# The wide matmuls of a two-layer decoder trunk walk their columns from the last to the first

## Chip, cores and metric

One core of one Trainium2 chip runs the whole program, two layers of a decoder trunk on a sequence of 256 tokens. The metric is device time in microseconds (us). Three runs of the kernel before took 861.75, 861.93 and 862.0 us.

## The reference

`x` is 256 x 1024 in float32. Each of two layers computes

```
h = RMSNorm(x)
[pool | diff-attn | stick-breaking | forgetting-attn | forget logits | gate logits] = h @ w_in      # 1024 x 7428
y_n = branch_n(...) @ w_branch[rows of branch n]                                                     # 1280 x 1024 in all
x = x + (sum_n sigmoid(gate_logit_n + b_gate_n) * y_n) @ w_out                                       # 1024 x 1024
x = x + (silu(gate) * up) @ w_down, with [gate | up] = RMSNorm(x) @ w_up                             # 1024 x 5632, 2816 x 1024
```

All weights are float32. The attention branches have four heads of 64 (the differential one four pairs, with values of 128).

## The kernel before

**Units.** The products with the five weight matrices are cut into items of up to 512 output columns, and the items into units: one unit is 2 x 128 weight rows by 512 columns (260 columns in the item `pf`). A layer has 144 units (`U`). The unit is the step of every pipeline: the load queue (SyncE) fetches it into one of 6 slots of `raw` (L562), ScalarE rounds it to the matmul's fp32r type in `w_hi` (L737), VectorE writes what the rounding left over into `w_lo` (L1013), both in rings of 5 slots, and TensorE multiplies it (`multiply`, L1668). Loads wait for `lo_ready` of the unit 6 earlier, ScalarE's copy waits for `unit_done` of the unit 5 earlier.

**Wide products.** The activations stand in SBUF turned (features on partitions) and split in the same manner into a rounded part and a rest (`hT`, `oT`, `aT`, each `_hi` and `_lo`). For each of the two weight row tiles of a unit and each of the two token tiles, `multiply` issues three matmuls into the same sums: high by high (L1692), high by low (L1693) and low by high (L1696). The activations are the stationary operand, 128 x 128, loaded anew for each matmul; the weights are streamed, and the output is 128 tokens by 512 columns of float32, a whole PSUM bank. `bulk` has four banks: two items by two token tiles, used in turn. The first four units, which start before all inputs are there, have their own order in `first_unit` (L1705), and the last unit's second token tile is done in two halves of 256 columns into the banks A and B (L1790 to L1792), so that the last additions and stores can start early.

**Order.** TensorE's order is written out by hand: before unit u the stages listed in `PE_TIMETABLE` run (transposes, attention scores, masks, sums), then the unit's twelve wide matmuls. Most units are multiplied singly; at four places four units are grouped so that all of tile 0 comes before tile 1. VectorE and ScalarE have tables of the same kind. They take the finished sums out of `bulk` after a semaphore that the last matmul of a unit or item raises (`unit_done`, `early_done`; for the residual sums L1057), and a bank is written afresh only after its reader's semaphore (`released_by`). At the end VectorE adds the two half banks to `x` (L1406) and ScalarE's queue stores the last piece (L996).

The small matmuls of the stages (transposes at L1441, L1634 and others, scores through `product_pair` at L1432, masks at L1576) are issued by lines of their own.

A bank's address comes from one line:

```python
        def item_bank(layer, n, t):
            return bulk[:, (layer * NITEM + n) % 2, t, :]
```

Of the kernel before, what the change touches and what calls it, by code (L numbers as in the profile page):

```python
# [32 lines left out]
P = 128  # L33
TT = 2
SEQ = TT * P
DEPTH = 2
D = 1024
KD = D // P
# [37 lines left out]
def item_k(n):  # L76
    k = ITEMS[n][3]
    return list(k) if not isinstance(k, int) else list(range(k))
# [23 lines left out]
U = len(UNITS)  # L102
# [207 lines left out]
def build(nc, x, attn_norm, ffn_norm, w_in, b_gate, w_branch, w_out, w_ffn_up, w_ffn_down, consts, params, turned_x, out):  # L310
# [8 lines left out]
    with ExitStack() as ctx:  # L319
        def sb(name, shape, dt=F32, stack=ctx, align=32):  # L320
            return stack.enter_context(nc.sbuf_tensor(name, shape, dt, align_bytes=align))
# [15 lines left out]
        def nth(semaphore, layer, event):  # L337

            order_in_layer = event_order[id(semaphore)]
            if layer == 0 and event in first_norm:  # L340
                return first_norm[event]
            return layer * len(order_in_layer) + order_in_layer[event] + more_in_first[id(semaphore)]
# [6 lines left out]
        w_hi = sb("w_hi", [P, RING, 2, NC], F32R, align=LINE)  # L349
        w_lo = sb("w_lo", [P, RING, 2, NC], F32R, align=LINE)  # L350

        x_sb = sb("x_sb", [P, TT, D])
        hT = [sb("hT_hi", [P, KD, SEQ], F32R, align=LINE), sb("hT_lo", [P, KD, SEQ], F32R, align=LINE)]
# [102 lines left out]
        def item_bank(layer, n, t):  # L456
            return bulk[:, (layer * NITEM + n) % 2, t, :]
# [76 lines left out]
        def released_by(name, t):  # L534

            return {
                "dq": (normed, ("dq", t)), "pf": (u_ready, t), "dk": (normed, ("dk", t)), "ss": (ss_staged, t),
                "svfq": (squares, ("fq", t)), "fkfv": (squares, ("fk", t)), "dv": (v_ready, ("dv", t)),
                "gate": (gate_ready, (name[1], t)), "branch": (gated, (*name[1:], t)),
                "out": (x_out, (t, name[1])), "down": (x_down, (t, name[1])),  # L540
                "ffg": (ff_gated, (name[1], t)), "ffu": (ff_ready, (name[1], t)), "fflast": (ff_ready, (NPAIR, t)),
            }[name if isinstance(name, str) else name[0]]
# [175 lines left out]
        def _(act):  # L718
# [226 lines left out]
            def nothing(*_):  # L945
                pass
# [463 lines left out]
        def _(pe):  # L1410
# [3 lines left out]
            def take(banks, *freed):  # L1414

                for b in banks:
# [2 lines left out]
                        pe.wait_ge(sig, nth(sig, layer, event))  # L1419
                    last_read[b] = freed  # L1420

            def product(dst, a, b, start, stop):

                pe.matmul(dst, a[0], b[0], start=start, stop=False, skip_group_check=True)
                pe.matmul(dst, a[0], b[1], start=False, stop=False, skip_group_check=True)
                return pe.matmul(dst, a[1], b[0], start=False, stop=stop, skip_group_check=True)
# [214 lines left out]
            def lhs_of(name, k, t):  # L1641

                kind = name if isinstance(name, str) else name[0]
                if kind == "branch":
                    event = (("pool", k) if k < 2 else ("diff", t) if k < 6 else ("sb", k - 6) if k < 8 else ("fox", k - 8))
                    return oT, event
                if kind == "down":
                    return aT, ("act", k // 4, t)
                if kind == "out":
                    return hT, ("merged", k // 4, t)  # L1650
                which = "ffn" if kind in ("ffg", "ffu", "fflast") else "attn"
                return hT, ("norm", which, t, k // 4)
# [9 lines left out]
            def wait_low(layer, event):  # L1662

                if nth(lhs_lo, layer, event) > reached["low"]:
                    reached["low"] = nth(lhs_lo, layer, event)
                    pe.wait_ge(lhs_lo, nth(lhs_lo, layer, event))

            def multiply(g, tiles, high=True, low=True):  # L1668

                layer, u = divmod(g, U)  # L1670
                n, k0 = UNITS[u]
                name, _, columns, _ = ITEMS[n]
                ks = item_k(n)
                width = sum(w for _, w in columns)
                fresh_bank = high and k0 == ks[0] and layer * NITEM + n >= 2
                before, m = divmod(layer * NITEM + n - 2, NITEM)
                for i in range(2):
                    k = k0 + i
                    whi, wlo = w_hi[:, g % RING, i, 0:width], w_lo[:, g % RING, i, 0:width]
                    for t in tiles:  # L1680
                        operand, event = lhs_of(name, k, t)
                        hi, lo = (part[:, k, t * P:(t + 1) * P] for part in operand)
                        dst = item_bank(layer, n, t)[:, 0:width]
                        if fresh_bank and i == 0:
                            sig, released = released_by(ITEMS[m][0], t)
                            pe.wait_ge(sig, nth(sig, before, released))
                        if high:
                            if low:
                                wait_low(layer, event)
                            else:  # L1690
                                wait_high(layer, event)
                            pe.matmul(dst, hi, whi, start=(k == ks[0]), stop=False)  # L1692
                            pe.matmul(dst, hi, wlo, start=False, stop=False)  # L1693
                        if low:
                            wait_low(layer, event)
                            ins = pe.matmul(dst, lo, whi, start=False, stop=(k == ks[-1] or g == DEPTH * U - 2 and i == 1 and t == 1))  # L1696
                if g == DEPTH * U - 2 and 1 in tiles:
                    ins.then_inc(all_but_last_done, 1)
                elif low and 1 in tiles:
                    ins.then_inc(unit_done, 1)  # L1700
                elif low and k == ks[-1]:
                    ins.then_inc(early_done, 1)


            def first_unit(u):  # L1705

                tiles = range(2 * u, 2 * u + 2)

                def high(k):

                    if k < 2:
                        pe.wait_ge(first_tile_hi, k + 1)
                    else:
                        pe.wait_ge(lhs_hi, k - 1)
                    if u < 2 and k == 2 * u:
                        pe.wait_ge(first_tile_ready, u + 1)
                    else:
                        pe.wait_ge(hi_ready, nth(hi_ready, 0, u))
                    for t in range(TT):
                        pe.matmul(item_bank(0, 0, t), hT[0][:, k, t * P:(t + 1) * P], w_hi[:, u, k % 2, :], start=(k == 0), stop=False)  # L1720

                def low(k):

                    pe.wait_ge(lhs_lo, k + 1)
                    for t in range(TT):
                        pe.matmul(item_bank(0, 0, t), hT[1][:, k, t * P:(t + 1) * P], w_hi[:, u, k % 2, :], start=False, stop=False)

                for k in tiles:
                    high(k)
                    if u < 2:  # L1730
                        low(k)
                if u >= 2:
                    for k in tiles:
                        low(k)
                pe.wait_ge(lo_ready, nth(lo_ready, 0, u))
                last = u == KD // 2 - 1
                for t in range(TT):
                    for k in tiles:
                        ins = pe.matmul(item_bank(0, 0, t), hT[0][:, k, t * P:(t + 1) * P], w_lo[:, u, k % 2, :], start=False,
                                        stop=k == KD - 1)  # L1740
                    if last and t == 0:
                        ins.then_inc(early_done, 1)
                ins.then_inc(unit_done, 1)
# [10 lines left out]
            for layer in range(DEPTH):  # L1754
                u = 0 if layer else GROUPS[0]
# [27 lines left out]
            for q in range(2):  # L1783
                columns = slice(q * NC // 2, (q + 1) * NC // 2)
                take("AB"[q], lhs_lo, DEPTH - 1, ("act", NPAIR, 1))
                dst = bank["AB"[q]][:, 0:NC // 2]
                for i in range(2):
                    hi, lo = (part[:, k0 + i, P:SEQ] for part in aT)
                    whi, wlo = w_hi[:, last % RING, i, columns], w_lo[:, last % RING, i, columns]
                    pe.matmul(dst, hi, whi, start=(i == 0), stop=False)  # L1790
                    pe.matmul(dst, hi, wlo, start=False, stop=False)
                    ins = pe.matmul(dst, lo, whi, start=False, stop=(i == 1))  # L1792
                ins.then_inc(last_columns_done, 1)


# [48 lines left out]
```

## Time and profile before

| | |
|---|---|
| median of three runs | 861.93 us (861.75 to 862.0) |
| span of the profiled execution | 859.8 us |
| the profiled execution's total | not given beside its span |
| granted TensorE clock, mean | 1.000 |
| busy: TensorE / weight loads / VectorE / ScalarE / GpSimd | 855.7 / 711.6 / 593.9 / 446.0 / 113.6 us |
| matmuls | 4246 |
| read from memory | 158.74 MB, 186 GB/s over the span |

The span goes from the first to the last instruction of one execution; the runs' times take in what lies around it. Busy time is time in which at least one instruction of an engine is in flight. A matmul's listed duration includes its way through the array, which overlaps the next matmul, so the rate of a dense stretch is read from the distance between starts. A granted clock of 1.000 stands for 2.4 GHz, 0.5 for 1.2 GHz.

### The profile page before, as it was taken

The page shows a single profiled execution, that of the slowest core. Times are in us where ns is not written, and L with a number is a line of the kernel's source. Part 1 is how long each engine was busy: PE and PEld are TensorE (multiplying, and loading weights), DVE is VectorE, ACT ScalarE, POOL GpSimd, SP SyncE. Part 2 cuts the span into 40 slices and gives each one's busy share as a digit, 9 for nine tenths or more (in the row PEclk, how much of TensorE's full clock was granted, in tenths as well). Part 3 has the DMA queues.
Part 4 walks back from the last instruction along what each step waited for, and adds up shares of the span by engine and source line. Part 5 has one row for each costly group of instructions (what it writes and reads, how often), then busy time and mean ns, then how long its engine had stood idle before and what let it go on. Part 6 is the DMA issues. An engine that isn't in the chain of part 4 may idle for free.

```text
span 859.8 us, 11140 instructions
## 1 busy us (share of the span) xinstructions
PE 855.7 (100%) x4246; PEld 711.6 (83%) x4246; DVE 593.9 (69%) x850; ACT 446.0 (52%) x646; POOL 113.6 (13%) x89
## 2 busy tenths in 40 slices
PE   9999999999999999999999999999999999999998
PEld 7888888888888888888888888888888888888887
DVE  7896967768777665564479768768696765565543
ACT  7567654854454444443364674558443644444431
POOL 0750101005401000000005401010063000000000
PEclk9999999999999999999999999999999999999999
DMA  9846656475657666555566465665665576665641
GB/s 343 290 150 190 200 175 183 148 228 180 188 184 236 190 195 190 182 185 189 162 186 178 119 195 158 196 197 162 205 196 179 151 234 183 185 190 177 195 147 50
DMA packets 87815, 160.53 MB, mean 187 GB/s; under 512 B 7505, under 2 KB 14161, under 8 KB 87761
## 3 DMA queue, kind: packets, MB, share of 16 engines
q1 hardware_dynamic: 87328, 159.16, 58.8%
q8 instruction: 34, 0.56, 0.3%
q10 hardware_dynamic: 432, 0.66, 0.2%
q14 instruction: 21, 0.16, 0.0%
HBM read 158.74 MB, written 1.05 MB: 186 GB/s over the span
## 4 chain that ended last, share of the span: by engine, by line
PE 93%; DVE 3%; DMA 2%; ACT 1%; SPq 1%; issue 0%; ACTq 0%
PE bulk L1692 28%; PE bulk L1696 28%; PE bulk L1693 28%; DMA raw<-in_w_in_dram 2%; DVE w_lo L1013 2%; PE bankAB L1432 1%; PE bankAB L1634 1%; PE bankT L1587 0%; PE bankAB L1576 0%; ACT w_hi L737 0%; PE bankAB L1441 0%; PE bankAB L1532 0%; PE bankO L1545 0%; PE bankT L1634 0%; PE bankO L1634 0%
## 5 line engine op out<-in xcount | busy, mean ns | idle before, releaser
L1013 DVE TENSOR_TENSOR w_lo<-raw,w_hi 128x1024 fp32r<-128x1024 f32 (+1 forms) x288 | 362.3, 1272 | 156.5 <-ACT w_hi L737 152.9
L737 ACT ACTIVATE w_hi<-raw 128x1024 fp32r<-128x1024 f32 (+1 forms) x286 | 297.7, 1049 | 245.3 <-PE bulk L1696 240.8
L1692 PE MATMUL bulk<-w_hi,hT_hi 128*128 128x512 f32 (+1 forms) x880 | 344.1, 391 | 0.2 <-DVE w_lo L1013 0.2
L1693 PE MATMUL bulk<-w_lo,hT_hi 128*128 128x512 f32 (+1 forms) x880 | 339.2, 385 | 0.0
L1696 PE MATMUL bulk<-w_hi,hT_lo 128*128 128x512 f32 (+1 forms) x880 | 336.5, 386 | 0.0
L1692 PEld LDWEIGHTS bulk<-w_hi,hT_hi 128*128 128x128 f32 x880 | 165.3, 188 | 33.2 <-DVE w_lo L1013 0.7
L1696 PEld LDWEIGHTS bulk<-w_hi,hT_lo 128*128 128x128 f32 x880 | 165.0, 188 | 33.4
L1693 PEld LDWEIGHTS bulk<-w_lo,hT_hi 128*128 128x128 f32 x880 | 165.4, 188 | 31.7
L1692 PE MATMUL bulk<-w_hi,aT_hi 128*128 128x512 f32 x174 | 68.0, 391 | 0.0
L1696 PE MATMUL bulk<-w_hi,aT_lo 128*128 128x512 f32 x174 | 67.7, 389 | 0.0
L1693 PE MATMUL bulk<-w_lo,aT_hi 128*128 128x512 f32 x174 | 67.7, 389 | 0.0
L709 POOL TENSOR_TENSOR wide<-wide 128x512 f32<-128x512 f32 x24 | 44.2, 1861 | 118.8 <-DVE wide L1309 118.4
L675 POOL TENSOR_TENSOR wide<-wide,ropeA 128x512 f32<-128x512 f32 x8 | 12.9, 1612 | 203.0 <-DVE wide L1116 202.9
L1696 PEld LDWEIGHTS bulk<-w_hi,aT_lo 128*128 128x128 f32 x174 | 32.7, 188 | 6.8
L1693 PEld LDWEIGHTS bulk<-w_lo,aT_hi 128*128 128x128 f32 x174 | 32.7, 188 | 6.7
L1692 PEld LDWEIGHTS bulk<-w_hi,aT_hi 128*128 128x128 f32 x174 | 32.7, 188 | 6.7
L1692 PE MATMUL bulk<-w_hi,oT_hi 128*128 128x512 f32 x80 | 31.3, 391 | 0.0
L1696 PE MATMUL bulk<-w_hi,oT_lo 128*128 128x512 f32 x80 | 31.2, 389 | 0.0
L1693 PE MATMUL bulk<-w_lo,oT_hi 128*128 128x512 f32 x80 | 31.1, 389 | 0.0
L935 ACT ACTIVATE wide<-bulk,y_ffn 128x512 f32<-128x512 f32 (+1 forms) x24 | 14.3, 649 | 18.2 <-PE bulk L1696 16.0
L1299 DVE SCALAR_TENSOR_TENSOR wide<-bulk,y_attn,bias 128x512 f32<-128x512 f32 x32 | 22.5, 745 | 0.7 <-PE bulk L1696 0.7
L1323 DVE SCALAR_TENSOR_TENSOR wide<-bulk,y_ffn,wide 128x512 f32<-128x512 f32 (+1 forms) x24 | 15.8, 702 | 10.2 <-ACT wide L935 10.2
(259 smaller groups left out, 720.7 us busy)
## 6 DMA issues: line engine op xcount, KB each, us to landing
raw<-in_w_in_dram SPq DMA_DIRECT2D x110, 512.0 KB, 4.1
raw<-in_w_ffn_up_dram SPq DMA_DIRECT2D x80, 512.0 KB, 4.4
raw<-in_w_ffn_down_dram SPq DMA_DIRECT2D x44, 512.0 KB, 3.3
raw<-in_w_branch_dram SPq DMA_DIRECT2D x20, 512.0 KB, 4.2
raw<-in_w_out_dram SPq DMA_DIRECT2D x16, 512.0 KB, 3.4
bias<-in_b_gate_dram SPq DMA_DIRECT2D x16, 256.0 KB, 4.4
raw<-in_w_ffn_up_dram SPq DMA_DIRECT2D x16, 256.0 KB, 3.2
raw<-in_w_in_dram SPq DMA_DIRECT2D x10, 256.0 KB, 2.7
```

What stands on the lines that cost most here:

```text
L675: pool.tensor_tensor(ta, x, ropeA[:, i, t:t + 1, :].broadcast_to([P, 8, HD]), ALU.mult)
L709: ins = pool.tensor_tensor(m, m, wide[:, t, n * D + j * NC:n * D + (j + 1) * NC], ALU.add)
L737: act.activation(w_hi[:, g % RING, :, 0:width], raw[:, g % RAW, :, 0:width], ACT.Copy).then_inc(hi_ready, 1)
L935: act.activation(ff_tmp(t, p, width), item_bank(layer, ITEM_AT[item], t)[:, 0:width], ACT.Sigmoid, scale=y_ffn[:, t:t + 1]).then_inc(ff_si ...
L1013: vec.tensor_tensor(w_lo[:, g % RING, :, 0:width], raw[:, g % RAW, :, 0:width], w_hi[:, g % RING, :, 0:width].bitcast(F32), ALU.subtract). ...
L1299: vec.scalar_tensor_tensor(out=wide[:, t, g * NC:(g + 1) * NC], in0=item_bank(layer, ITEM_AT[("gate", g)], t), scalar=y_attn[:, t:t + 1], ...
L1323: vec.scalar_tensor_tensor(out=s, in0=item_bank(layer, ITEM_AT[item], t)[:, 0:width], scalar=y_ffn[:, t:t + 1], in1=s, op0=ALU.mult, op1=A ...
L1432: ins = pe.matmul(dst, a[a_part], b[b_part], start=start and a_part + b_part == 0, stop=stop and a_part == 1, skip_group_check=True)
L1634: ins = pe.transpose(bank[name][:, k * P:(k + 1) * P], ff_act(t, p, blocks * P)[:, k * P:(k + 1) * P], identity)
L1692: pe.matmul(dst, hi, whi, start=(k == ks[0]), stop=False)
L1693: pe.matmul(dst, hi, wlo, start=False, stop=False)
L1696: ins = pe.matmul(dst, lo, whi, start=False, stop=(k == ks[-1] or g == DEPTH * U - 2 and i == 1 and t == 1))
```

## The change

A helper `backward` turns the free axis of the output and of the streamed operand of a matmul, so that the columns are streamed from the last to the first and the sums are written from the last to the first. It replaces `pe.matmul` at all nine lines of the wide products, in `multiply`, in `first_unit` and in the split last unit. Stationary operands, flags, waits and semaphores are as before, and so are the small matmuls.

```diff
+            def backward(dst, stationary, streamed, start, stop):
+
+                return pe.matmul(dst[:, ::-1], stationary, streamed[:, ::-1], start=start, stop=stop)
+
...
-                            pe.matmul(dst, hi, whi, start=(k == ks[0]), stop=False)
-                            pe.matmul(dst, hi, wlo, start=False, stop=False)
+                            backward(dst, hi, whi, start=(k == ks[0]), stop=False)
+                            backward(dst, hi, wlo, start=False, stop=False)
                         if low:
                             wait_low(layer, event)
-                            ins = pe.matmul(dst, lo, whi, start=False, stop=(k == ks[-1] or g == DEPTH * U - 2 and i == 1 and t == 1))
+                            ins = backward(dst, lo, whi, start=False, stop=(k == ks[-1] or g == DEPTH * U - 2 and i == 1 and t == 1))
...
-                        pe.matmul(item_bank(0, 0, t), hT[0][:, k, t * P:(t + 1) * P], w_hi[:, u, k % 2, :], start=(k == 0), stop=False)
+                        backward(item_bank(0, 0, t), hT[0][:, k, t * P:(t + 1) * P], w_hi[:, u, k % 2, :], start=(k == 0), stop=False)
...
-                        pe.matmul(item_bank(0, 0, t), hT[1][:, k, t * P:(t + 1) * P], w_hi[:, u, k % 2, :], start=False, stop=False)
+                        backward(item_bank(0, 0, t), hT[1][:, k, t * P:(t + 1) * P], w_hi[:, u, k % 2, :], start=False, stop=False)
...
-                        ins = pe.matmul(item_bank(0, 0, t), hT[0][:, k, t * P:(t + 1) * P], w_lo[:, u, k % 2, :], start=False,
-                                        stop=k == KD - 1)
+                        ins = backward(item_bank(0, 0, t), hT[0][:, k, t * P:(t + 1) * P], w_lo[:, u, k % 2, :], start=False,
+                                       stop=k == KD - 1)
...
-                    pe.matmul(dst, hi, whi, start=(i == 0), stop=False)
-                    pe.matmul(dst, hi, wlo, start=False, stop=False)
-                    ins = pe.matmul(dst, lo, whi, start=False, stop=(i == 1))
+                    backward(dst, hi, whi, start=(i == 0), stop=False)
+                    backward(dst, hi, wlo, start=False, stop=False)
+                    ins = backward(dst, lo, whi, start=False, stop=(i == 1))
```

## Rows read from the trace of the kernel before

**Rows 1.** Span and clock of the core; the page's busy time, clock and chain.

```profile
core 0: 859.8 us, clock 1.000
...
PE 855.7 (100%) x4246; PEld 711.6 (83%) x4246; DVE 593.9 (69%) x850; ACT 446.0 (52%) x646; POOL 113.6 (13%) x89
...
PEclk9999999999999999999999999999999999999999
...
PE 93%; DVE 3%; DMA 2%; ACT 1%; SPq 1%; issue 0%; ACTq 0%
PE bulk L1692 28%; PE bulk L1696 28%; PE bulk L1693 28%; DMA raw<-in_w_in_dram 2%; DVE w_lo L1013 2%; PE bankAB L1432 1%; PE bankAB L1634 1%; PE bankT L1587 0%; PE bankAB L1576 0%; ACT w_hi L737 0%; PE bankAB L1441 0%; PE bankAB L1532 0%; PE bankO L1545 0%; PE bankT L1634 0%; PE bankO L1634 0%
```

**Rows 2.** Waits of TensorE: in total, times, longest, all in us.

```profile
PE bulk L1748 <- DVE warm L1358: 1.0, 1, 1.0
PE bulk L1720 <- ACT w_hi L973: 0.3, 1, 0.3
PE bulk L1692 <- DVE w_lo L1013: 0.2, 1, 0.2
```

**Rows 3.** Waits of ScalarE, VectorE and the load queue, the longest of each.

```profile
ACT w_hi L737 <- PE bulk L1696: 240.8, 162, 6.2
...
DVE w_lo L1013 <- ACT w_hi L737: 152.9, 120, 4.7
...
SPq L562 <- DVE w_lo L1013: 686.1, 280, 11.6
```

**Rows 4.** Time line of TensorE at the end: start us, us, line, operation.

```profile
844.61 0.39 PE L1692 MATMUL bulk<-w_hi,aT_hi 128*128 128x512 f32 x1
844.84 0.39 PE L1693 MATMUL bulk<-w_lo,aT_hi 128*128 128x512 f32 x1
845.07 0.39 PE L1696 MATMUL bulk<-w_hi,aT_lo 128*128 128x512 f32 x1
...
855.27 0.39 PE L1696 MATMUL bulk<-w_hi,aT_lo 128*128 128x512 f32 x1
855.49 0.28 PE L1790 MATMUL bankAB<-w_hi,aT_hi 128*128 128x256 f32 x1
855.61 0.28 PE L1791 MATMUL bankAB<-w_lo,aT_hi 128*128 128x256 f32 x1
...
856.81 0.28 PE L1792 MATMUL bankAB<-w_hi,aT_lo 128*128 128x256 f32 x1
```

**Rows 5.** TensorE's groups by shape: busy us, mean ns; L1693, L1696 count alike.

```profile
L1692 PE MATMUL bulk<-w_hi,hT_hi 128*128 128x512 f32 x848 | 334.8, 395 | 0.2 <-DVE w_lo L1013 0.2
...
L1692 PE MATMUL bulk<-w_hi,aT_hi 128*128 128x512 f32 x174 | 68.0, 391 | 0.0
...
L1692 PE MATMUL bulk<-w_hi,oT_hi 128*128 128x512 f32 x80 | 31.3, 391 | 0.0
...
L1692 PE MATMUL bulk<-w_hi,hT_hi 128*128 128x260 f32 x32 | 9.3, 292 | 0.0
...
L1720 PE MATMUL bulk<-w_hi,hT_hi 128*128 128x512 f32 x16 | 4.8, 401 | 0.3 <-ACT w_hi L973 0.3
...
L1790 PE MATMUL bankAB<-w_hi,aT_hi 128*128 128x256 f32 x4 | 1.1, 282 | 0.0
```

**Rows 6.** Chain in order of time around eight transposes, and their weight loads.

```profile
273.51 0.23 PE bulk L1696
273.75 0.88 PE bankAB L1634 x8
274.62 0.24 PE bulk L1692
274.86 0.23 PE bulk L1693
...
273.35 1.03 PEld L1634 LDWEIGHTS bankAB<-con,wide 128*128 128x128 f32 x8
```

**Rows 7.** A bank read by VectorE (ns min/median/max), and the time line's end.

```profile
L1057 DVE TENSOR_TENSOR x_sb<-bulk,x_sb x15: 684/684/692, 236.9 to 854.3; 128x512 f32<-128x512 f32 x15
...
857.12 0.42 DVE L1406 TENSOR_TENSOR x_sb<-bankAB,x_sb 128x256 f32<-128x256 f32 x1 [0.22 <-PE bankAB L1792]
857.58 0.35 ACTq L996 DMA_DIRECT2D out_dram<-x_sb  x1
```

## The prediction

> **What bounds the kernel now.** I read the core's span and clock and the page's first part, then the chain of waits, then the groups by shape, then TensorE's own time line where nothing but wide products runs. The first shows TensorE with a matmul in flight for 855.7 of 859.8 us, at a granted clock of 1.000, the 2.4 GHz level, throughout [rows 1]. That busy time counts overlapping matmuls once, so alone it does not prove that TensorE sets the pace. The chain does: 93% of it is TensorE, and 84% the three wide products of `multiply` (28% each of L1692, L1693 and L1696) [rows 1]. TensorE's own waits come to 1.5 us in the whole span, all in the start or at single places [rows 2]. Everybody else waits for it: ScalarE's weight copies 240.8 us for L1696, VectorE behind those 152.9 us, and the load queue 686.1 us behind VectorE [rows 3]. So a nanosecond on each wide matmul appears in full in the time, and there is nothing ahead of TensorE that could hide or shorten it.
>
> The price of one wide matmul has to be its start-to-start distance, since the listed 389 ns overlap. In the last stretch 48 matmuls of 512 columns start between 844.61 and 855.49 us: 10.88 / 48 = 226.7 ns. The twelve of 256 columns start from 855.49 to 856.81, eleven distances, 120.0 ns each [rows 4]. The difference, 106.7 ns for 256 columns, is 0.4168 ns a column, one column per cycle of 2.4 GHz, and what is left, 226.7 - 213.4 = 13.3 ns, is fixed per matmul. So nearly everything is streaming, which is just what the change touches.
>
> **How much is touched.** By shape there are 848 + 174 + 80 matmuls of 512 columns at each of three lines and 16 at each of the three lines of `first_unit`: 3 x 1118 = 3354. To these come 3 x 32 = 96 of 260 columns and 3 x 4 = 12 of 256 [rows 5]. Together 3462 instructions and 3354 x 512 + 96 x 260 + 12 x 256 = 1,745,280 columns. At 0.4168 ns these are 727.4 us, and 3462 x 13.3 ns add 46.0 us: 773 of the 859.8 us, 90%. The small matmuls (scores, transposes, masks) keep their order.
>
> **The change part by part.** It adds and removes no instruction, wait, transfer or buffer. Order on every engine stays, each accumulation meets the same partners in the same order (column c is still the sum of the same products), the semaphores still go up when a whole matmul is done, and VectorE and ScalarE read whole banks after that. Three things can have a price.
>
> First, the walk of the streamed operand (`w_hi`, `w_lo`) down instead of up. No row of the trace shows a descending walk, so I bound it. The low end is 0: the walk still touches neighbours, each once, and the weights for it were written long before. The high end is from the nearest row with a slower walk on the same engine: the eight transposes of 128 columns at 273.75 us take 0.88 us, 110 ns each, and each needs a fresh load of 128 columns of 4 bytes [rows 6], so 0.86 ns a column, about twice the 0.4168 of the stream. That is one column per cycle of 1.2 GHz instead of 2.4. A stream that falls to this half rate costs another 727.4 us. I take 0, since the stream touches the same neighbours at the same distance, and a fixed distance between neighbours is all that a pattern tells the engine; half rate would need hardware that treats one sign on its own.
>
> The Trainium skill (SBUF — State Buffer, in the section on the DMA port swizzle, its note on SBUF "cachelines") says that accesses to one 16-byte line run at full bandwidth and that a line needs at least two hits. A descending walk has four fp32 hits a line like an ascending one, so by this rule the read costs 0 and the sum stays as it is. No run here shows it.
>
> Second, the walk of the sums down through the PSUM bank. Same ends, 0 and 727.4 us (one half-rate walk covers the other if both fall to it). I take 0 with less confidence than for the read, because the add into a sum is a read and a write per column at 2.4 GHz, where hardware has more reason to take neighbours in pairs, and a pair in falling order may not be taken as one.
>
> Third, the turn itself: each matmul begins at the far end. If decoding or the hand-over from one matmul to the next grows, it is at most of the size of the 13.3 ns that are there: 0 to 46.0 us. Within a run of wide products each begins where its predecessor also began, so I take 0. At the borders to the small, still ascending matmuls (0.88 us for the eight transposes, then the first wide one with 0.24 us in the chain against 0.23 [rows 6]) there is no room for more than some hundredths of a us each.
>
> On the other engines: VectorE reads a 512-column bank in 684 ns [rows 7], and it starts on the semaphore of the whole matmul, so it neither gains from the order of columns nor collides otherwise. The end is unchanged: last matmul starts at 856.81, VectorE adds at 857.12 and ScalarE's queue stores at 857.58 [rows 7]. The sum: 859.8 + 0 + 0 + 0 = 859.8 us of span. The median of the runs is 861.93, 2.1 us over the span; the profiled execution has no separate total, so I take these 2.1 us as what lies around it. Forecast 861.9 us.
>
> **The rivals.**
>
> *Half rate (slower).* One of the two walks, more likely the write into `bulk`, runs at one column per cycle of 1.2 GHz when it descends. Place: every wide matmul. Price: 1,745,280 x 0.4168 ns = 727.4 us, since TensorE waits for nobody and hides nothing: 861.9 + 727.4 = 1589 us. It decides as soon as the 512-column distance is 440 ns instead of 227. Against it: no added work, same neighbours. For it: the column rate is at the top level of the clock, so there is no reserve, and the load row shows that this engine does take 4-byte columns at half that rate in another path [rows 6].
>
> The Trainium skill backs this rival (Advanced Engine Details and Errata, PSUM Cachelines): lines there are two fp32 values and "Any non-contiguous AP significantly slows down matmuls". It gives no figure, and its next sentence asks only that every two consecutive elements be contiguous, which two falling neighbours are in one sense and not in the other. By the strict reading the time is this rival's, by the mild one the forecast's; no trace here shows either.
>
> *A price of the turn (slower).* The fixed part doubles at most: +46.0 us, 908 us; a third of that still gives 877. For it: 13.3 ns is not nothing, so something happens between matmuls. Against: no row has a pattern-dependent gap, 512 and 256 columns show the same one.
>
> *The hand-over shrinks (faster).* If part of the 13.3 ns comes from the start of a bank, the other end might avoid it, down to 861.9 - 46.0 = 816 us. Nothing speaks for it.
>
> *The change doesn't do what it says.* Both patterns of a matmul are turned together, which is mathematically the same matmul; if the program is rewritten to ascending ones on the way to the chip, the time is 861.9 whatever the hardware would do.
>
> **How the numbers follow.** Measurement tells this kernel from no change at about 0.2%, 1.7 us, or half a nanosecond per wide matmul. Direction without effect 0.46, undone on the way 0.08: together 0.54 for 861.9, with a range of its own of 861 to 863.5. Half rate 0.34; slower still (both walks one after the other, or under half rate) 0.02; turn price 0.07; faster 0.03. So faster 0.03, same 0.54, slower 0.43. Up to 908 us the cases hold only 0.61 to 0.64, so the range must reach half rate: 861 to 1600 us (1589 and some for borders), which leaves out about 0.05.
>
> **What would show it.** In the changed profile: distances in the last stretch, 226.7 ns (forecast), 440 (half rate), up to 240 (turn price: then 256 columns lie above 120.0 by the same amount, while half rate adds 107 ns to them and 213 to 512). The granted clock must stay at 1.000; if it falls, my sum lacks a term. The transposes must stay at 0.88 us for eight. In the half-rate case ScalarE's, VectorE's and the load queue's waits grow by about the added time. A slower kernel at an unchanged distance, from new waits on VectorE or ScalarE, would prove the reasoning wrong altogether.

## The result and the profile after

The changed kernel takes 881.7 us (881.32 to 881.81) where the kernel before takes 861.9 us: ratio 1.023, 95% interval 1.0209 to 1.025. That is 19.8 us slower. Its profiled execution has a span of 879.5 us, 19.7 more than [rows 1].

The core's span and clock, then the page's busy time and its chain:

```profile
core 0: 879.5 us, clock 1.000
```

```profile
PE 875.8 (100%) x4246; PEld 712.6 (81%) x4246; DVE 594.8 (68%) x850; ACT 446.0 (51%) x646; POOL 109.6 (12%) x89
...
PE 100%; DVE 0%; issue 0%
PE bulk L1424 91%; PE bankAB L1436 2%; PE bankAB L1638 1%; PE bulk L1752 1%; PE bankT L1591 0%; PE bankAB L1580 0%; PE bankAB L1536 0%; PE bankAB L1445 0%; PE bankO L1549 0%; PE bankT L1638 0%; PE bankO L1638 0%; PE bankO L1609 0%; PE bankO L1602 0%; PE bankO L1603 0%; PE bankO L1601 0%; PE bankAB L1454 0%
```

The granted clock is 1.000 as in [rows 1], so a lower clock is not the reason. The chain is now TensorE to 100%, and 91% of it is the helper's line L1424, which stands for all nine lines of before. Nothing has been put ahead of TensorE: the added time is inside its own work.

TensorE's time line at the end, against [rows 4]:

```profile
861.88 0.40 PE L1424 MATMUL bulk<-w_hi,aT_hi 128*128 128x512 f32 x1
...
874.95 0.40 PE L1424 MATMUL bulk<-w_hi,aT_lo 128*128 128x512 f32 x1
875.18 0.28 PE L1424 MATMUL bankAB<-w_hi,aT_hi 128*128 128x256 f32 x1
...
876.48 0.28 PE L1424 MATMUL bankAB<-w_hi,aT_lo 128*128 128x256 f32 x1
```

From 861.88 to 875.18 us 57 matmuls of 512 columns start: 13.30 / 57 = 233.3 ns each, against 226.7. The eleven distances of 256 columns take 1.30 us, 118.2 ns each, against 120.0. So there is a price on each matmul of 512 columns and none at 256: neither the fixed price of my "turn" rival, which would stand at both widths, nor one in proportion to the columns.

The chain in the middle, against [rows 6], and the waits behind TensorE, against [rows 3]:

```profile
272.78 6.07 PE bulk L1424 x26
278.85 0.87 PE bankAB L1638 x8
```

```profile
ACT w_hi L737 <- PE bulk L1424: 254.9, 164, 6.4
...
DVE w_lo L1013 <- ACT w_hi L737: 161.8, 119, 5.1
```

26 matmuls take 6.07 us, 233.5 ns each, also where loads and splits go on beside them; the transposes still take 0.87 us for eight. ScalarE waits 254.9 us for TensorE instead of 240.8, VectorE 161.8 behind it instead of 152.9: both have more time left over. Of 3354 matmuls of 512 columns each loses 19.7 us / 3354 = 5.9 ns on average, less than the 6.6 ns of the steady stretches. The rest is at the borders: from 22 us on, the first dozen distances between starts in each row of wide matmuls behind a small stage grow from 236.5 to 240.7 ns on average, all later ones from 226.7 to 233.3. There are 694 of the first kind and 2532 of the second, together 19.7 us.

### The profile page after: what moved, and what is told of

Its sections match the earlier page's. It is cut to its first block, busy times and chain, and to the rows that moved or that the text cites. A ratio compares the mean times of both kernels' runs of the same rounds, so it can differ in the third digit from the quotient of the medians.

```text
span 879.5 us, 11140 instructions
## 1 busy us (share of the span) xinstructions
PE 875.8 (100%) x4246; PEld 712.6 (81%) x4246; DVE 594.8 (68%) x850; ACT 446.0 (51%) x646; POOL 109.6 (12%) x89
## 4 chain that ended last, share of the span: by engine, by line
PE 100%; DVE 0%; issue 0%
PE bulk L1424 91%; PE bankAB L1436 2%; PE bankAB L1638 1%; PE bulk L1752 1%; PE bankT L1591 0%; PE bankAB L1580 0%; PE bankAB L1536 0%; PE bankAB L1445 0%; PE bankO L1549 0%; PE bankT L1638 0%; PE bankO L1638 0%; PE bankO L1609 0%; PE bankO L1602 0%; PE bankO L1603 0%; PE bankO L1601 0%; PE bankAB L1454 0%
## 5 line engine op out<-in xcount | busy, mean ns | idle before, releaser
L1013 DVE TENSOR_TENSOR w_lo<-raw,w_hi 128x1024 fp32r<-128x1024 f32 (+1 forms) x288 | 363.1, 1273 | 165.9 <-ACT w_hi L737 161.8
L737 ACT ACTIVATE w_hi<-raw 128x1024 fp32r<-128x1024 f32 (+1 forms) x286 | 297.5, 1048 | 259.3 <-PE bulk L1424 254.9
L1424 PE MATMUL bulk<-w_hi,hT_hi 128*128 128x512 f32 (+1 forms) x896 | 355.5, 399 | 0.0
L1424 PE MATMUL bulk<-w_lo,hT_hi 128*128 128x512 f32 (+1 forms) x896 | 350.6, 394 | 0.0
L1424 PE MATMUL bulk<-w_hi,hT_lo 128*128 128x512 f32 (+1 forms) x896 | 347.6, 394 | 0.0
L1424 PEld LDWEIGHTS bulk<-w_hi,hT_hi 128*128 128x128 f32 x896 | 168.3, 188 | 38.7 <-issue 0.9
L1424 PEld LDWEIGHTS bulk<-w_hi,hT_lo 128*128 128x128 f32 x896 | 168.2, 188 | 38.7
L1424 PEld LDWEIGHTS bulk<-w_lo,hT_hi 128*128 128x128 f32 x896 | 168.6, 188 | 37.3 <-DVE w_lo L1013 0.4
L1424 PE MATMUL bulk<-w_hi,aT_hi 128*128 128x512 f32 x174 | 69.4, 399 | 0.0
L1424 PE MATMUL bulk<-w_hi,aT_lo 128*128 128x512 f32 x174 | 69.2, 397 | 0.0
L1424 PE MATMUL bulk<-w_lo,aT_hi 128*128 128x512 f32 x174 | 69.1, 397 | 0.0
L709 POOL TENSOR_TENSOR wide<-wide 128x512 f32<-128x512 f32 x24 | 41.7, 1760 | 124.9 <-DVE wide L1309 124.4
L1424 PEld LDWEIGHTS bulk<-w_hi,aT_lo 128*128 128x128 f32 x174 | 32.7, 188 | 7.9
L1424 PEld LDWEIGHTS bulk<-w_lo,aT_hi 128*128 128x128 f32 x174 | 32.7, 188 | 7.8
L1424 PEld LDWEIGHTS bulk<-w_hi,aT_hi 128*128 128x128 f32 x174 | 32.7, 188 | 7.7
L1424 PE MATMUL bulk<-w_hi,oT_hi 128*128 128x512 f32 x80 | 32.0, 399 | 0.0
L1424 PE MATMUL bulk<-w_lo,oT_hi 128*128 128x512 f32 x80 | 31.8, 397 | 0.0
L1424 PE MATMUL bulk<-w_hi,oT_lo 128*128 128x512 f32 x80 | 31.8, 397 | 0.0
```

Source lines behind the costliest of these rows:

```text
L709: ins = pool.tensor_tensor(m, m, wide[:, t, n * D + j * NC:n * D + (j + 1) * NC], ALU.add)
L737: act.activation(w_hi[:, g % RING, :, 0:width], raw[:, g % RAW, :, 0:width], ACT.Copy).then_inc(hi_ready, 1)
L1013: vec.tensor_tensor(w_lo[:, g % RING, :, 0:width], raw[:, g % RAW, :, 0:width], w_hi[:, g % RING, :, 0:width].bitcast(F32), ALU.subtract). ...
L1424: return pe.matmul(dst[:, ::-1], stationary, streamed[:, ::-1], start=start, stop=stop)
```

## The experiments

**1. Read or write.** The helper turned one operand at a time:

```diff
-                return pe.matmul(dst[:, ::-1], stationary, streamed[:, ::-1], start=start, stop=stop)
+                return pe.matmul(dst, stationary, streamed[:, ::-1], start=start, stop=stop)      # read only
+                return pe.matmul(dst[:, ::-1], stationary, streamed, start=start, stop=stop)      # write only
```

> The changed kernel with only the streamed weights walked from the last column to the first; the sums are written in rising order, so the columns of every wide product come out mirrored (what the rest computes with is other data, the work is the same). Changed kernel 881.7 us, 233.3 ns between wide matmuls of 512 columns against 226.7 before. Theory A (the read of the weights is what costs): 881 to 882 us, 233.3 ns. Theory B (the write of the sums costs): 862 us, 226.7 ns. Theory C (either costs something, or only both together): between 862 and 882 us or the full 862 us here and in the write-only run.

> The changed kernel with only the sums written from the last column to the first; the weights are streamed in rising order, so the columns of every wide product come out mirrored. Theory A (read): 862 us, 226.7 ns between wide matmuls of 512 columns. Theory B (write): 881 to 882 us, 233.3 ns. Theory C (both together, or a share each): 862 us here and in the read-only run, or a share of the 20 us in each.

Read only: 881.5 us, ratio 1.023 (1.0215 to 1.0245). Write only: 861.6 us, ratio 1.000 (0.999 to 1.0009). The chain from 300 us on, read only and then write only:

```profile
299.94 2.33 PE bulk L1424 x10
```

```profile
299.95 12.24 PE bulk L1424 x54
```

Ten matmuls in 2.33 us are 233 ns each, 54 in 12.24 us are 226.7. The whole price is the read's; writing a PSUM bank from its end adds nothing (861.6 us). Theory A holds within 0.3 us, B and C fall.

**2. Matmuls by themselves.** A kernel of groups of 48 matmuls, tiles and slots cycled as in a unit, one line per pattern. Each of the four kernels of groups in this document was run once, so a group's time is one reading:

```python
            for h, w, d, s, k, t, part, u, i, z in ops():
                pe.matmul(d[:, ::-1], h, w[:, ::-1], start=s, stop=z)
```

> A kernel of its own: groups of 48 wide matmuls with nothing beside them (no weights are loaded or split meanwhile), the operands cycled as in a unit, one group per pattern: both walks, read only, write only, widths from 128 to 510 columns in both directions, the two halves of 256 swapped, falling inside halves, falling inside or between groups of four columns, and bf16. The rest of the decoder is left out. If the cost comes from traffic of other engines (loads, splits), 512 columns show no difference between directions here (226.7 ns each). If it is TensorE's own, 233.3 against 226.7 ns stands here too. A fixed price of the turn would show as the same difference at every width, 6.6 ns; a price per column as a difference in proportion to the width (3.3 ns at 256). The read-only and write-only groups must agree with the runs of the whole kernel. If swapped halves with rising columns inside already cost 6.6 ns, it is where the walk starts and not its sign.

Its chain shows for each group its start, its length and its count. L84 is rising at 512 columns, L86 both falling, L88 read only, L90 write only; L102 and L104 are 256 columns rising and falling, L114 and L116 384 columns; L152 and L154 are bf16, rising and falling:

```profile
46.48 10.88 PE bulk L84 x48
57.36 11.21 PE bulk L86 x48
68.56 11.20 PE bulk L88 x48
79.76 10.89 PE bulk L90 x48
...
122.95 5.78 PE bulk L102 x48
128.73 5.68 PE bulk L104 x48
...
159.96 8.32 PE bulk L114 x48
168.28 8.54 PE bulk L116 x48
...
345.00 10.38 PE bulk L152 x48
355.38 10.36 PE bulk L154 x48
```

Divided by 48: 226.7, 233.5, 233.3 and 226.9 ns. The price is there with nothing going on beside TensorE, and again it is the read's. By width, falling less rising: 512 columns 6.9 ns, 384 columns 4.6, 320 columns 0.2, 256 columns -2.1. It is no fixed price and no price per column. In bf16 (two bytes an element) both directions take 216 ns: there the price does not exist. Two halves of 256 swapped with rising columns inside took 10.92 us for 48 (227.5 ns), halves in order with falling columns inside 11.21 (233.5): where the walk begins is of no account.

**3. Which neighbours must rise.** In the whole kernel, the read in groups of four columns, the sums written rising:

```diff
-                return pe.matmul(dst[:, ::-1], stationary, streamed[:, ::-1], start=start, stop=stop)
+                def fours(ap):
+
+                    return ap.rearrange("p (a b) -> p a b", b=4)
+
+                return pe.matmul(fours(dst), stationary, fours(streamed)[:, :, ::-1], start=start, stop=stop)   # falling inside
+                return pe.matmul(fours(dst), stationary, fours(streamed)[:, ::-1, :], start=start, stop=stop)   # groups falling
```

> The changed kernel with the streamed weights read in groups of four neighbouring columns (16 bytes), the groups rising and the four inside each falling, sums written rising, so that only four neighbours of every product come out swapped among themselves. If the step of minus one column costs: 881 us. If only the order of the 16-byte groups counts, as the groups of the kernel of its own say (226.9 ns): 862 us.

> The opposite: groups of four from the last to the first, the four inside rising, sums written rising. If the step of minus one column costs: 862 us. If the order of the 16-byte groups counts: 881.5 us, 233.3 ns between wide matmuls of 512 columns.

Falling inside each four: 861.8 us, ratio 1.000 (0.9991 to 1.0009); groups of four falling, 881.6 us, ratio 1.0232 (1.0214 to 1.0249). The step of minus one column is free. What costs is the order of the 16-byte groups.

**4. What the loaded tile has to do with it.** Groups of 512 columns again:

> The kernel of groups again, now varying the tile that is loaded for each matmul while the one before streams: 128, 64 or 32 columns of it, the same tile each time, every second column, its start shifted by 4 to 256 columns, the stream's start shifted, bf16; each with the stream rising and falling, 48 matmuls of 512 columns. [...] Theory E (a falling walk costs by itself, whatever is loaded): the difference stays 6.6 ns at 64 and 32 columns and at every shift.

The question behind the widths is whether a stream and the load of the next tile meet. If they do, and each direction pays for it in proportion to what is loaded, the time over the 213.3 ns of pure streaming (13.3 ns rising, 20.0 falling) should fall to a quarter at 32 columns.

L84 and L86 are rising and falling with 128 loaded columns, L92 and L94 with 64, L96 and L98 with 32. L106 is falling with the tiles in another buffer, L108 the rising group behind it with the tiles moved by 4 columns; L120 and L122 are rising and falling with the tiles moved by 32:

```profile
47.39 10.88 PE bulk L84 x48
58.27 11.21 PE bulk L86 x48
...
91.88 11.04 PE bulk L92 x48
102.91 11.20 PE bulk L94 x48
114.11 11.12 PE bulk L96 x48
125.23 11.20 PE bulk L98 x48
...
169.44 11.21 PE bulk L106 x48
180.64 11.20 PE bulk L108 x48
...
247.85 11.16 PE bulk L120 x48
259.00 11.51 PE bulk L122 x48
```

Falling is 233.3 to 233.5 ns at all three widths of the tile. Rising is 226.7 with 128 loaded columns, 230.0 with 64 and 231.7 with 32. So neither direction gets cheaper with a smaller load, and theory E falls as well, since the difference shrinks to 3.3 and 1.7 ns. The rising stream also goes to 233.3 ns when the tiles are moved by 4, 8 or 16 columns, and to 232.5 at 32, but stays at 227.1 at 64 or 256; the falling one goes up to 239.8 at 32. My reading from here on, theory F: 226.7 ns is a favoured case, in which a rising stream and the loaded tile suit each other, and the falling walk loses it. The 239.8 ns show that the place of the tile can cost a falling stream as well.

**5. The tiles moved in the whole kernel.** `hT`, `oT` and `aT` each became one tensor for both parts, with its start moved by 4 or 32 columns:

```diff
-        hT = [sb("hT_hi", [P, KD, SEQ], F32R, align=LINE), sb("hT_lo", [P, KD, SEQ], F32R, align=LINE)]
+        def shifted(name, blocks, stack=ctx):
+
+            whole = sb(name, [P, 2 * blocks * SEQ + 4], F32R, stack, LINE)
+            return [whole[:, 4 + i * blocks * SEQ:4 + (i + 1) * blocks * SEQ].rearrange("p (k q) -> p k q", q=SEQ) for i in range(2)]
+
+        hT = shifted("hT", KD)
```

> The kernel before, columns rising, with the activations that are loaded as stationary tiles (hT, oT, aT) placed 4 columns (16 bytes) further, so that no tile starts at a multiple of 64 columns. Theory F (226.7 ns is a favoured case, in which a rising stream and a loaded tile that starts at a multiple of 64 columns suit each other; the falling stream merely loses it): 233.5 ns between wide matmuls as in the kernel of groups, and 881 to 884 us with no column turned. Theory E (the falling step itself costs, the place of the tile is of no account in the kernel): 862 us.

> The kernel before with the loaded tiles placed 32 columns further. Theory F, by the group with that shift (232.5 ns): 862 + 3354 x 5.8 ns, 879 to 882 us. Theory E: 862 us.

> The changed kernel (columns falling) with the loaded tiles placed 4 columns further. Theory F: the falling stream has nothing left to lose at this shift, 233.3 ns and 881.7 us, the same as the changed kernel, so that direction makes no difference any more. Theory E (the falling walk has a price of its own on top of any other): above 881.7 us by what the rising kernel loses, some 902 us. It is also the check that placing the buffers anew costs nothing by itself.

> The changed kernel with the loaded tiles placed 32 columns further, where the groups showed 239.8 ns for a falling stream against 232.5 for a rising one. Theory F, in its full form (both reads share the buffer's time in a pattern that place and direction set together): 881.7 + 3354 x 6.5 ns, 902 to 904 us. If the place is of no account in the kernel: 881.7 us.

Rising, moved by 4: 866.7 us, ratio 1.0059 (1.0044 to 1.0074), a quarter of what theory F said. Rising, moved by 32: 878.7 us, 1.0196 (1.0181 to 1.0211), just under the 879 to 882 of F. Falling, moved by 4: 881.4 us, 1.0228 (1.0213 to 1.0243), as F said and unlike E, so placing the buffers anew costs nothing of itself. Falling, moved by 32: 882.2 us, 1.0236 (1.0219 to 1.0253), where the groups had led me to 902: a miss.

The chain of the rising kernel moved by 4, in two stretches, tells why it lies between:

```profile
272.96 0.23 PE bulk L1697
...
275.30 0.24 PE bulk L1698
...
329.36 0.23 PE bulk L1697
...
331.85 0.23 PE bulk L1701
```

From 272.96 to 275.30 us ten matmuls start, 234 ns each; from 329.36 to 331.85 eleven, 226 ns each. Same instructions, same places, two speeds. The whole trace says when it changes. It has 36 rows of wide matmuls between small stages with more than two dozen in them. Leaving out the first dozen of each, 22 rows run at 227 ns throughout, 13 at 233, and one, at the start, changes inside. So the rate is set where a row begins and then stays, up to 234 matmuls long.

**6. Block size, other orders, memory of the state.**

> The kernel of groups a third time. (1) At which size a falling order begins to cost: blocks of 8 to 128 columns from the last to the first with rising columns inside, and the reverse. Known so far: blocks of 4 falling 233.3 ns, halves of 256 swapped 227.5, four falling inside rising groups 226.9, 256 falling inside rising halves 233.5. If what counts is the way the stream walks while the next tile is loaded, blocks falling cost 233.3 up to some size and 227 from there, and falling inside costs from some size on. (2) Whether any other order of reading is cheaper than the rising one: 2 to 32 parts of the row interleaved by 4 to 64 columns. If the 13.3 ns over the 213.3 of pure streaming come from two reads that meet, some order should come below 226.7 ns; if they are the hand-over from matmul to matmul, none does. (3) 96 loaded columns: by the proportion seen at 128, 64 and 32 (rising 226.7, 230.0, 231.7, falling 233.3 at all) rising gives 228.3 ns, falling 233.3. (4) Tiles shifted by 4 columns with the rest operands in a tensor of their own, as in the whole kernel, after a falling and after a rising group: if the pattern remembers what came before, the two differ.

L92 is blocks of 8 falling with rising columns inside, L98 blocks of 64; L104 and L108 are blocks of 16 and of 64 rising with falling columns inside; L114, L128 and L134 interleave 2, 8 and 32 parts of the row by 4 columns; L136 is rising with 96 loaded columns. L140 and L146 are rising with tiles moved by 4 columns, L140 behind a falling group of 96 loaded columns and L146 behind a rising group; L148 is falling with such tiles:

```profile
71.44 11.20 PE bulk L92 x48
...
105.00 10.93 PE bulk L98 x48
...
137.99 12.80 PE bulk L104 x48
...
162.16 11.20 PE bulk L108 x48
...
195.45 12.01 PE bulk L114 x48
...
276.46 13.35 PE bulk L128 x48
...
313.13 10.86 PE bulk L134 x48
323.99 11.04 PE bulk L136 x48
...
346.24 10.88 PE bulk L140 x48
...
378.88 10.88 PE bulk L146 x48
389.76 11.21 PE bulk L148 x48
```

Falling blocks cost 6.6 ns at 8 columns, 5.8 at 32, and next to nothing from 64 on (227.7 on average, and 226.7 at 128). Falling inside costs 6.6 ns at 64, and at 16 columns it gives 266.7 ns, 40 more than rising. 96 loaded columns gave 230.0, not 228.3, so the saving is not in proportion to what is loaded.

Interleaving shows that rising inside each block of 64 is not enough. With 2 and 8 parts by 4 columns the groups of every block are still met in rising order, but the stream changes block after each group: 250.2 and 278.1 ns. Two parts interleaved by whole blocks of 64 take 227.3. One description fits the orders of whole groups tried so far: what counts is the sequence of places modulo 64 columns. Whole blocks can change their order without changing it, and falling along the row or inside blocks of 64 gives the same sequence and the same time (233.5 and 233.3 ns). Two parts interleaved visit each place twice running, eight parts eight times. It is a description, and no run shows what stands behind it.

L146 is the same pattern as L108 of experiment 4: 226.7 ns here behind a rising group, 233.3 there behind a falling one. But my test of that in this kernel missed: L140, behind a falling group, stays at 226.7 from its first matmul, as the same tiles do behind a rising group. So what ran before matters, and "falling" alone does not say which rate follows.

**7. The block of 64 in the whole kernel, and each group from the same state.**

```diff
-                return pe.matmul(dst[:, ::-1], stationary, streamed[:, ::-1], start=start, stop=stop)
+                width = dst.shape[-1]
+                if width % 64:
+                    return pe.matmul(dst, stationary, streamed, start=start, stop=stop)
+                blocks = [ap.rearrange("p (a b) -> p a b", b=64)[:, ::-1, :] for ap in (dst, streamed)]         # e_blocks64
+                blocks = [ap.rearrange("p (a b) -> p a b", b=64)[:, :, ::-1] for ap in (dst, streamed)]         # e_in64
+                return pe.matmul(blocks[0], stationary, blocks[1], start=start, stop=stop)
```

> Groups of 48 matmuls of 512 columns, each behind a group in the plain rising order, so that all start from the same state. Tiles placed 4 to 56 columns further, streams placed 4 to 48 further, more interleaved orders, neighbouring groups of 4 to 32 columns swapped, and at the end a rising group straight behind a falling one. If the state is remembered, tiles +4 to +16 stay at 226.7 ns here, where they stood at 233.5 behind a falling group; if the place alone decides, they show 233.5 again. The rising group behind the falling one: back at 226.7 within some six matmuls, as before. If the time over 213.3 ns is waiting of two reads for one another, some order goes below 226.7 (64 or 32 parts interleaved by 4 are the candidates, 219 to 227); if it is the hand-over, none does.

> The changed kernel with blocks of 64 columns from the last to the first, the columns inside each block rising, read and write alike (the 96 matmuls of 260 columns stay plainly rising). By the groups (227 ns in the steady state): 862 to 864 us, though the walk starts at the far end and falls from block to block. If the overall direction counts: 881 us.

> The reverse: blocks of 64 columns from the first to the last, the columns inside each falling. By the groups (233.3 ns): 881 to 882 us. If the overall direction counts: 862 us.

Blocks falling, columns inside rising: 861.7 us, ratio 0.9999 (0.9989 to 1.0009). Blocks rising, columns inside falling: 881.5 us, 1.0229 (1.0213 to 1.0245). Their chains from 300 us on, in this order:

```profile
300.00 12.01 PE bulk L1428 x53
```

```profile
299.85 2.80 PE bulk L1428 x12
```

53 matmuls in 12.01 us, 226.6 ns; 12 in 2.80 us, 233.3 ns. The groups, each behind a rising one: L86 tiles moved by 4, L90 by 8, L142 32 parts interleaved by 4, L166 neighbouring groups of 8 columns swapped, L184 rising straight behind a falling group:

```profile
58.47 10.88 PE bulk L86 x48
...
80.23 11.19 PE bulk L90 x48
...
366.92 10.74 PE bulk L142 x48
...
499.39 12.80 PE bulk L166 x48
...
600.58 10.89 PE bulk L184 x48
```

Moved by 4 the rising stream keeps 226.7 ns if it had it; moved by 8 it loses it also behind a rising group. Moving the stream instead of the tile costs too: 231.7 ns at 4 columns, 233.3 at 8, 229.2 at 16, 233.1 at 32. One order is below 226.7: 10.74 / 48 = 223.8 ns. The same order is L134 of experiment 6, where it stood behind an interleaved group and took 226.3. Behind a falling group the rising one is at 226.9 on average, so it finds its state again within a few matmuls. Swapping neighbours of 8 columns costs 40 ns a matmul.

**8. The cheaper order in the whole kernel.** Four columns from each of 32 parts of 16 columns, then the next four of each:

```diff
-                return pe.matmul(dst[:, ::-1], stationary, streamed[:, ::-1], start=start, stop=stop)
+                if dst.shape[-1] % 64:
+                    return pe.matmul(dst, stationary, streamed, start=start, stop=stop)
+                return pe.matmul(combed(dst), stationary, combed(streamed), start=start, stop=stop)
+
+            def combed(ap):
+
+                return ap.rearrange("p (a b c) -> p b a c", b=4, c=4)
```

> All wide products but the 96 of 260 columns take their columns four at a time from each of the 32 (at 256 columns 16) neighbouring parts of 16 columns, then the next four of each, read and write alike, so the sums are the same. By the groups 223.8 ns in place of 226.7, if the write's order is free: 861.7 - 3354 x 2.9 ns = 852 us. If a write in pieces of four columns costs, slower than the read-only run. If the gain of the groups needs an undisturbed row of 48, 857 to 862 us.

> The same order for the read alone, the sums written in rising order, so that the columns of the wide products come out in another order. 852 us by the groups, which were written this way; 857 to 862 us if the small matmuls between the units take the gain away. Against the run with read and write alike it prices the order of the write.

Read and write: 857.7 us (856.72 to 858.88), ratio 0.9956 (0.9943 to 0.9968). Read only: 857.4 us, 0.9949 (0.9934 to 0.9965). So it beats both kernels, by 3.9 us over the one before, less than half of the 9.7 us of the groups. The chain tells where the rest goes. First read and write, in two stretches, then read only from 300 us on:

```profile
299.91 12.28 PE bulk L1426 x55
...
374.31 48.72 PE bulk L1426 x215
```

```profile
299.94 12.24 PE bulk L1426 x54
```

55 matmuls take 12.28 us, 223.3 ns each; the 215 from 374.31 us on take 226.6 ns, and in the read-only run the stretch at 300 us takes 226.7. Of the 36 long rows of wide matmuls, 9 run at 223 ns in the first run and 8 in the second. Nearly all others lie between 225 and 228 ns. So this order, too, has two rates. 857.7 us lies in the band that I gave for a gain that needs an undisturbed row, but that is not the reason: undisturbed rows of over 200 matmuls are without the gain.

Writing the sums in pieces of four columns, 64 bytes apart, is 0.3 us slower than writing them in order, inside the spread of the runs (2.2 us).

## Why the prediction was wrong

**The bound.** Right: TensorE sets the pace and nothing hides its work: 6.6 ns on 3354 matmuls would be 22.1 us, and 19.8 us appear in the time. Order, waits, buffers and clock are as said, and so are the transposes and the end.

**The step that failed** is the first of the three prices, the falling read, "I take 0". It measured 19.8 us, all of the result, 2.7% of the upper end of 727.4 us that I had set beside it. My reason, that a fixed distance between neighbours is all a pattern tells the engine, looked at the stream alone. The runs show 6.6 ns on a steady 512-column matmul instead of 0. It comes from the order of the 16-byte groups: turned as whole blocks of 64 columns they cost nothing (861.7 us), turned inside these blocks they cost all of it (881.5 us). The price also changes with the place and width of the tile that is loaded meanwhile. [rows 6] had shown that loads and streams overlap, and I used that row only as a slow rate.

**The row behind it.** I split 226.7 ns into 213.4 of streaming and a fixed 13.3 of hand-over. That was the deeper error: two widths cannot show that a remainder is fixed. It moved from 13.3 to 20 ns with the order at 512 columns, to about 10 ns in the combed order's faster rows, and is under 3 ns in bf16, so most of it is no fixed hand-over. Had I asked what it consists of, a small price on the read would have had a place and a size of its own.

**The second price,** the falling write, at 0: right, and shown alone. **The third,** the turn, at 0: right, 256 columns got no slower. My rival of that name had the right size, up to 46.0 us, in the wrong place: its mark, the same addition at 256 columns, is absent. **Half rate** had a chance of 0.34 and did not occur. **Undone on the way:** excluded, since the read shows.

**The rules.** The Trainium skill (SBUF — State Buffer, the note on SBUF "cachelines") says that consecutive accesses to one 16-byte line run at full bandwidth, with at least two hits a line; a falling read has four, from which I took a price of 0. The runs agree inside a line (861.8 us when the four fall) and not between lines: with all four columns of each line read in sequence the order of the lines alone makes 226.7, 233.3 or 266.7 ns. The Trainium skill (Advanced Engine Details and Errata, PSUM Cachelines) says that any non-contiguous pattern slows matmuls significantly. Here neither a falling write nor one in pieces of four columns costs anything that the runs can tell, so the strict reading does not hold for these two.

**The numbers.** 881.7 lies between my likeliest case (861 to 863.5) and half rate, among the times of the turn price, to which I gave 0.07 and whose mechanism did not occur. The forecast of no change was wrong. That 861 to 1600 us holds the time is luck: it reached so far only for half rate, and no case of mine was a price on the read of this size.

**What stays open.** That a load and a stream meet in SBUF would fit the type (4 bytes), the place of the tile modulo 64 columns and the two rates that last, but it is argued and not shown: every matmul here has a load of its own, none streams without one, and in which order the tile itself is read could not be varied. What picks the rate at the start of a row was not found. Why 32 loaded columns leave a rising stream at 231.7 ns and not nearer to pure streaming, and why the falling kernel moved by 32 columns took 882 and not 902 us, is not explained.

## What to carry to other kernels

In a kernel that is bound by 4-byte matmuls of full width, the order in which the streamed columns are read and the place of the loaded tile are worth a look: here they cost up to 2.4% of the kernel and gained 0.5%. Read the 16-byte groups rising inside 256 bytes and finish each 256 bytes before the next, start tiles and streams on multiples of 256 bytes, and measure a candidate in the whole kernel: groups of 48 promised 9.7 us for the combed order, and 3.9 came. The order of the write was free here, in both patterns tried. And what is left over after bytes or columns by rate is a term to be explained before it is called fixed.

## What the runs showed of the hardware

- A 512-column fp32r matmul with a 128-column load costs 226.7 ns rising and 233.3 falling; bf16 216 either way. At 320 columns the directions are alike, at 256 falling is 2 ns cheaper.
- The order inside four columns is free (861.8 us), and so is the order of whole blocks of 64 (861.7 us); columns falling inside blocks of 64 give 881.5 us.
- Place matters: loaded tiles moved by 8 columns 233.3 ns, by 64 columns 227.1; all tiles of the kernel moved by 32 columns 878.7 us.
- A rate lasts: with tiles moved by 16 bytes the same 48 matmuls take 10.88 us behind a rising group and, in one case of two, 11.20 behind a falling one. In the whole kernel with such tiles 35 of 36 long rows keep 227 or 233 ns from their second dozen on.
- Swapping neighbours of 8 columns costs 40 ns a matmul (266.7), interleaving 8 parts by 4 columns 51 (13.35 us for 48, 278.1 ns); interleaving 32 parts by 4 gains 2.9 (223.8) behind a rising group and 0.4 (226.3) behind an interleaved one.
